# Depthwise convolution of a decoder trunk on TensorE: two tiles as diagonal products, or four tiles as packs of 32 channels by 4 shifts between the projection's chunks

## The chip, the cores and the metric

The kernel runs on one core of a Trainium2 chip. The metric is the device time of one execution in microseconds (us). The profile is one execution recorded by the hardware profiler; its rows name the engines PE (TensorE), PEld (TensorE's weight loads), DVE (VectorE), ACT (ScalarE), POOL (GpSimd) and SP (the queue that issues most transfers).

## The reference

There are two layers over 512 tokens of width 1024; only the first layer's branch matters here.

```python
def conformer_conv_branch(h, w_in, b_in, conv_w, conv_b, norm_g, norm_b, w_out, b_out):
    proj = h @ w_in + b_in                       # 1024 -> 3 x 2048
    val, glu_gate, z = jnp.split(proj, 3, axis=-1)
    u = val * jax.nn.sigmoid(glu_gate)
    u = lax.conv_general_dilated(u, conv_w[:, None, :], window_strides=(1,),
        padding=[(CONV_KERNEL - 1, 0)], dimension_numbers=('NWC', 'WIO', 'NWC'),
        feature_group_count=CONV_WIDTH) + conv_b # 31 taps, each channel by itself
    u = jax.nn.silu(layer_norm(u, norm_g, norm_b))
    u = u * jax.nn.silu(z)
    return u @ w_out + b_out
```

The rest (the residual's LayerNorm, then a latent attention layer with its projections) is the same in both kernels.

## The kernel before, in words

Data lie with channels on the 128 partitions and the 512 tokens along the row. The 2048 channels of the branch are 16 tiles `t` of 128 x 512; `u` holds them with 30 zero columns ahead (`PAD`).

**Chunks on PE.** One chunk `c` is 128 output columns of `w_in`: 24 matmuls of 128x512, since each float32 product is made of three (weights low part by data high, high by low, high by high). Chunks 0 to 31 alternate value (even) and gate (odd) of tiles 0 to 15, so tile `t` is complete after chunk 2t+1. Chunks 32 to 47 are z, called z0 to z15 below. A chunk's weights come by a transfer of SP into one of two `w_raw` slots, ACT rounds them to `w_hi`, POOL subtracts to get `w_lo` (`split_lo`), and PE waits for both. A `w_raw` slot is free when its `w_hi` and `w_lo` are made. After a gate chunk ACT makes `val` and `sig` and POOL multiplies them into `u` (`glu`).

**The convolution** of 31 taps per tile is dealt out to three places:

- DVE does the tiles in `VECTOR_TILES` (0, 1, 2, 4, 5, 6, 7, 8, 10, 11, 14, 15), one instruction a tap, two tiles in turn, with the partial sum in a PSUM bank; and the last 10 taps of tile 12.
- PE does 21 taps of tile 12 and all 31 of tile 13 (`convolve(m)`), each tap as a product with a diagonal matrix: 52 taps of 3 matmuls, all of them between chunk 31 and z0. POOL makes the high diagonals (`diag_hi`), ACT the low ones.
- Tiles 3 and 9 (`SHARED_TILES`) are multiplied tap by tap on ACT (`tap_product`) and added on POOL (`add_product`): 62 taps, dealt out over the steps of both engines.

**The mean.** The LayerNorm over channels needs the sum of all tiles. POOL sums 11 tiles (`pool_csum`), DVE the others, and when `csum` is ready PE multiplies it by ones after the sixth of the eight parts of z11 (`MEAN_AT = (11, 5)`, `sum_over_channels`). The rest of PE's queue stands behind that matmul. The sum of squares follows inside z14.

Every engine runs its own instructions in the order written and waits on semaphores; there is no scheduler. `tap_done` counts DVE's taps, and `whole_at()` says at which count a tile is whole.

Of the kernel before, what the change touches and what calls it, by code (L numbers as in the profile page):

```python
# [26 lines left out]
F32 = mybir.dt.float32  # L27
F32R = mybir.dt.float32r
# [12 lines left out]
PAD = TAPS - 1  # L41
N_HEADS = 16
# [71 lines left out]
def trunk_kernel(nc, x, positions, ln_g, ln_b, a_w_in, a_b_in, a_conv_w, a_conv_b, a_norm_g,  # L114
# [14 lines left out]
    with ExitStack() as ctx:  # L129
# [67 lines left out]
        cu_hi = [at(f"cu_hi{i}", reg_x, 4 * TILE + 544 * i, [P, SEQ + PAD], F32R) for i in range(2)]  # L197
        cu_lo0 = at("cu_lo0", reg_x, 4 * TILE + 1088, [P, SEQ + PAD], F32R)
# [7 lines left out]
        vec_raw = at("vec_raw", reg_acc, 4 * TILE, [V_ALL, P])  # L206
        pos_int = at("pos_int", reg_x, 8 * TILE - 512, [P, SEQ], I32)
# [5 lines left out]
        diag_hi = at("diag_hi", reg_z, 0, [P, TAPS, P], F32R)  # L213
        diag_lo = at("diag_lo", reg_z, TAPS * P, [P, TAPS, P], F32R)
# [95 lines left out]
        taps_hi_ready, taps_lo_ready, taps_ready = sem("taps_hi_ready"), sem("taps_lo_ready"), sem("taps_ready")  # L310
# [76 lines left out]
        SHARES_BEGIN = SHARED_TILES[0] + 2  # L387
# [61 lines left out]
        SECOND_BEGINS = 14  # L449
        POOL_SUM_BEGINS = 8  # L450
        POOL_SUM = MATRIX_TILES[1:] + SHARED_TILES + VECTOR_TILES[:8]

        def whole_at():

            first_tap = {t: 0 for t in VECTOR_TILES}
            first_tap[MATRIX_TILES[0]] = MATRIX_TAPS[0]
            coming, running, taken, done, slot, ends = list(first_tap), [None, None], [0, 0], 0, 0, {}
            while coming or running != [None, None]:
                if running[slot] is None and coming and (slot == 0 or done >= SECOND_BEGINS):
                    running[slot] = coming.pop(0)  # L460
                    taken[slot] = first_tap[running[slot]]
                if running[slot] is not None:
                    taken[slot] += 1
                    done += 1
                    if taken[slot] == TAPS:
                        ends[running[slot]] = done
                        running[slot] = None
                slot = 1 - slot
            return ends

        def pair_taps(t):

            n = max(0, t - SHARES_BEGIN)
# [1612 lines left out]
```

## Time and profile before

| | |
|---|---|
| median of 3 runs | 820.56 us (820.43 to 822.16) |
| span of the profiled execution, first to last instruction | 818.7 us |
| time of the profiled execution beside its span | the profile states none; the median lies 1.86 us above the span |
| PE / DVE / ACT / POOL busy, of the span | 99% / 74% / 48% / 66% |
| granted TensorE clock, mean | 0.999 of full |

The span is counted from the first instruction, and all times below are from there. The busy time of a PE matmul includes its drain, which overlaps the next one: the distance between the starts of two matmuls is shorter than the mean duration in a row.

### The profile page before, as it was taken

To read this page: it belongs to the slowest core of one execution; us is meant where nothing else is said; L and a number is where in the kernel's file an instruction comes from. 1 tells how busy PE (TensorE), PEld (TensorE's weight loads), DVE (VectorE), ACT (ScalarE), POOL (GpSimd) and SP (SyncE) were. 2 spreads that over 40 slices of the span, in tenths; PEclk is the share of its full clock that TensorE was granted. 3 is DMA by queue.
4 is the path that set the end of the run, shared out by engine and by line. 5 is a ranking of instruction groups with operands and counts; after the bars stand their busy time and mean duration, and the time that the engine had idled before them with its cause. 6 is when DMAs were issued, how large, how long until landed. Compare 5 with 4: busy or idle time off the path is not lost.

```text
span 818.7 us, 11442 instructions
## 1 busy us (share of the span) xinstructions
PE 807.0 (99%) x3891; PEld 681.3 (83%) x3891; DVE 602.9 (74%) x1026; ACT 395.5 (48%) x711; POOL 542.3 (66%) x335
## 2 busy tenths in 40 slices
PE   8999999999999999999999999999999999999996
PEld 8888888888888887888898788888888888888885
DVE  2699999999999978994833192037788888876217
ACT  4654444455564368622342444256666766664210
POOL 4677999995999954594355438426877776387430
PEclk9999999999999999999999999999999999999999
DMA  6333333330032324444233335115766664663412
GB/s 221 103 103 103 92 88 87 93 104 26 25 105 84 109 79 146 157 160 129 52 107 114 101 102 167 54 41 176 206 200 191 201 199 130 186 205 129 155 52 102
DMA packets 123019, 100.01 MB, mean 122 GB/s; under 512 B 15354, under 2 KB 107616, under 8 KB 122972
## 3 DMA queue, kind: packets, MB, share of 16 engines
q1 hardware_dynamic: 122972, 99.42, 40.4%
q8 instruction: 25, 0.41, 0.2%
q14 instruction: 22, 0.18, 0.1%
HBM read 82.36 MB, written 12.58 MB: 116 GB/s over the span
## 4 chain that ended last, share of the span: by engine, by line
PE 95%; DMA 2%; DVE 1%; ACT 0%; issue 0%; SPq 0%; DVEq 0%
PE bank L1694 91%; DMA x_in<-in_x_dram 1%; PE bank L1999 1%; PE bank L2000 1%; DMA prob_kept<-prob 1%; DMA prob_moved<-prob_kept 0%; PE bank L1873 0%; PE bank L1992 0%; DVE prob L1591 0%; PE bank L1926 0%; PE bank L1990 0%; PE bank L1808 0%; DVE prob L1596 0%; SPq L524 0%; ACT bank L1201 0%
## 5 line engine op out<-in xcount | busy, mean ns | idle before, releaser
L730 POOL TENSOR_TENSOR w_lo<-w_raw,w_hi 128x1024 fp32r<-128x1024 f32 x102 | 252.6, 2485 | 114.1 <-ACT w_hi L927 106.8
L1330 DVE SCALAR_TENSOR_TENSOR bank<-u,conv_w,bank 128x512 f32<-128x512 f32 x357 | 238.6, 747 | 0.5
L1694 PE MATMUL bank<-xt_hi,w_lo 128*128 128x512 f32 (+1 forms) x392 | 151.9, 388 | 0.0
L1694 PE MATMUL bank<-xt_hi,w_hi 128*128 128x512 f32 (+1 forms) x392 | 150.9, 385 | 0.0
L927 ACT ACTIVATE w_hi<-w_raw 128x1024 fp32r<-128x1024 f32 x102 | 106.3, 1054 | 92.2 <-PE bank L1694 29.8
L1694 PE MATMUL bank<-xt_lo,w_hi 128*128 128x512 f32 (+1 forms) x392 | 150.8, 385 | 0.0
L1694 PEld LDWEIGHTS bank<-xt_lo,w_hi 128*128 128x128 f32 x392 | 73.7, 188 | 15.0 <-issue 0.5
L1694 PEld LDWEIGHTS bank<-xt_hi,w_lo 128*128 128x128 f32 x392 | 73.7, 188 | 15.0 <-issue 0.5
L1694 PEld LDWEIGHTS bank<-xt_hi,w_hi 128*128 128x128 f32 x392 | 73.6, 188 | 14.7
L767 POOL TENSOR_TENSOR acc<-acc,tap_product 128x512 f32<-128x512 f32 x60 | 77.8, 1297 | 9.7 <-ACT tap_product L960 4.5
L1694 PE MATMUL bank<-ht_hi,w_lo 128*128 128x512 f32 (+1 forms) x208 | 76.4, 367 | 0.0
L1694 PE MATMUL bank<-ht_lo,w_hi 128*128 128x512 f32 (+1 forms) x208 | 75.8, 365 | 0.0
L1694 PE MATMUL bank<-ht_hi,w_hi 128*128 128x512 f32 (+1 forms) x208 | 75.8, 365 | 0.0
L886 POOL TENSOR_TENSOR pt_lo<-prob_moved,pt_hi 128x512 fp32r<-128x512 f32 (+1 forms) x64 | 57.7, 935 | 15.4 <-ACT pt_hi L1208 15.1
L855 POOL TENSOR_TENSOR bundle_lo<-bundle_raw,bundle_hi 128x1024 fp32r<-128x1024 f32 (+1 forms) x16 | 49.2, 3073 | 26.4 <-ACT bundle_hi L1135 26.4
L960 ACT ACTIVATE tap_product<-u,conv_w 128x512 f32<-128x512 f32 x60 | 42.0, 719 | 30.8 <-POOL acc L767 30.8
L1694 PE MATMUL bank<-w_hi,fg_lo 128*128 128x512 f32 x128 | 50.1, 391 | 0.7 <-issue 0.7
L1694 PE MATMUL bank<-w_hi,g_lo 128*128 128x512 f32 x128 | 50.1, 392 | 0.3 <-DVE g_lo L1422 0.3
L1694 PE MATMUL bank<-w_lo,g_hi 128*128 128x512 f32 x128 | 49.8, 389 | 0.0
L1694 PE MATMUL bank<-w_hi,g_hi 128*128 128x512 f32 x128 | 49.8, 389 | 0.0
L1694 PE MATMUL bank<-w_lo,fg_hi 128*128 128x512 f32 x128 | 49.8, 389 | 0.0
L1694 PE MATMUL bank<-w_hi,fg_hi 128*128 128x512 f32 x128 | 49.8, 389 | 0.0
(213 smaller groups left out, 1722.0 us busy)
## 6 DMA issues: line engine op xcount, KB each, us to landing
w_raw<-in_a_w_in_dram SPq DMA_DIRECT2D x48, 512.0 KB, 3.7
w_raw<-in_b_w_in_dram SPq DMA_DIRECT2D x20, 512.0 KB, 3.6
prob_kept<-prob SPq DMA_DIRECT2D x16, 640.0 KB, 3.1
prob_moved<-prob_kept SPq DMA_DIRECT2D x64, 160.0 KB, 3.2
w_raw<-in_a_w_out_dram SPq DMA_DIRECT2D x16, 512.0 KB, 4.0
w_raw<-in_b_w_out_dram SPq DMA_DIRECT2D x16, 512.0 KB, 3.5
bundle_raw<-in_b_w_uq_dram SPq DMA_DIRECT2D x16, 256.0 KB, 4.4
x_in<-in_x_dram SPq DMA_DIRECT2D x4, 512.0 KB, 5.8
```

The lines of the kernel that those rows point to most:

```text
L730: nc.gpsimd.tensor_tensor(w_lo[slot][:], w_raw[raw][:], w_hi[slot][:].bitcast(F32), ALU.subtract).then_inc(w_lo_ready, 1)
L767: nc.gpsimd.tensor_tensor(acc[:, t, :], acc[:, t, :], tap_product[n % 2][:], ALU.add).then_inc(product_added, 1)
L855: nc.gpsimd.tensor_tensor(bundle_lo[slot][part][:], bundle_raw[:, lo:hi], bundle_hi[slot][part][:].bitcast(F32), ALU.subtract).then_inc(bu ...
L886: nc.gpsimd.tensor_tensor(turned_block(pt_lo, b), moved_block(b), turned_block(pt_hi, b).bitcast(F32), ALU.subtract).then_inc(pt_lo_ready, 1)
L927: nc.scalar.activation(w_hi[slot][:], w_raw[raw][:], ACT.Copy).then_inc(w_hi_ready, 1)
L960: nc.scalar.activation(tap_product[n % 2][:], u[:, t, k:k + SEQ], ACT.Copy, scale=tap).then_inc(product_ready, 1)
L1330: nc.vector.scalar_tensor_tensor(out=inner[:] if k < TAPS - 1 else acc[:, t, :], in0=u[:, t, k:k + SEQ], scalar=conv_w[:, column:column + ...
L1694: last = nc.tensor.matmul(out_ap, a, b, start=(start and n == 0 and m == 0), stop=(stop and n == len(parts) - 1 and m == 2))
L1999: nc.tensor.matmul(total, stack[:, cut], keys(kr_lo[:]), start=False, stop=False)
L2000: nc.tensor.matmul(total, stack[:, cut], keys(kr_hi[:]), start=False, stop=True).then_inc(scores_done, 1)
```

## The change: four tiles on PE in packs, eleven on DVE, one shared

`MATRIX_TILES` becomes 1, 5, 9, 13, `SHARED_TILES` becomes 3 alone, and DVE has the other eleven tiles whole.

A tile on PE is cut into four packs of 32 channels. The 128 rows of the moving operand are those 32 channels at 4 successive shifts, so one matmul holds 4 taps of 32 channels for each of 4 column groups, which are 4 parts of the 31 taps. A pack takes two windows (`STEPS`), each with three matmuls; four packs make 24 matmuls a tile, 96 in all. They run in two halves of 12 after chunks 13 and 14, 21 and 22, 29 and 30, and z5 and z6.

To get the stacked rows, ACT rounds the tile to `cu_hi`, POOL makes `u_lo`, SP writes both to DRAM (`keep_u`) and reads them back in 8 transfers onto 32 partitions each (`stack_u`). POOL makes two matrices a tile (`pack_matrices`, 128x1024 each). ACT copies the packs out of PSUM and, from its own queue, writes them to DRAM (`keep_packs`), then brings three parts into the rows of `u` tiles 0, 2 and 4, whose taps are done, and the fourth into `acc` (`bring_parts`). DVE adds the three parts at their shifts onto `acc` (`add_part`, 3 instructions a tile): for the first three tiles after its taps 150, 222 and 294, for the last after all taps.

DVE splits tiles 0, 2, 4, 6 and 15 (`ALONE`) into taps 0 to 15 and 16 to 30, run in turn, and one addition joins them (`join_halves`). The chunk loops of PE and SP are written out. The two rounded tables of taps (`conv_w_hi`, `conv_w_lo`) are gone; four more transposes on PE after chunk 2 give the taps of the packs.

```diff
-        MATRIX_TILES = (12, 13)
-        MATRIX_TAPS = (21, TAPS)
+        MATRIX_TILES = tuple(range(MATRIX_COLUMN, CT, CT // TAP_ROWS))
+        BEGINS = (3, 7, 11, 15)
+        PACK_BANK = (6, 7)
-        SHARED_TILES = (3, 9)
+        SHARED_TILES = (3,)
-        PAIR_SHARE, MATRIX_SHARE, Z_SHARE = 3, (1, 1, 1, 9), 2
+        PAIR_SHARE = {6: 3, 7: 2, 8: 3, 10: 3, 11: 2, 12: 3, 14: 3, 15: 2}
+        Z_SHARE = {0: 2, 1: 2, 4: 2, 5: 2, 6: 2}
+        ALONE = (0, 2, 4, 6, 15)
+        ADD_PARTS_AT = (150, 222, 294)
...
+            def stack_after(c):
+                for m, begin in enumerate(BEGINS):
+                    n = c - 2 * begin
+                    if n == 3:
+                        keep_u(m)
+                    elif n in (5, 6):
+                        stack_u(m, 0, (0, 1) if n == 5 else (2, 3))
+                    elif n in (7, 8):
+                        stack_u(m, 1, (0, 1) if n == 7 else (2, 3))
...
@@ POOL, the z chunks @@
                 split_lo(Z0 + i, i % 2, i % SLOTS)
                 if i == 0:
                     glu(CT - 1, (CT - 1) % 2)
-                    for g in range(SHARED_SLOTS):
-                        conv_matrices(1, g)
-                        for n in matrix_taps(g):
-                            add_product(n)
+                if i in (2, 3):
+                    pack_matrices(len(MATRIX_TILES) - 1, i - 2)
                 for n in z_taps(i):
                     add_product(n)
...
@@ ACT @@
+            def bring_parts(m):
+                for i in range(2):
+                    act.wait_ge(part_written[i], 16 * (PACKS // 2) * (m + 1))
+                act.wait_ge(tap_done, whole_at()[PART_TILES[-1]])
+                wait(act, parts_added, (PARTS - 1) * m)
+                nc.scalar.dma_start(u[:, PART_TILES[0]:PART_TILES[-1] + 1:2, PAD:], parts_kept[m][0:PARTS - 1].rearrange("q p i -> p q i")
+                                    ).then_inc(parts_landed, 16)
+                nc.scalar.dma_start(acc[:, MATRIX_TILES[m], :], parts_kept[m][PARTS - 1]).then_inc(parts_landed, 16)
...
@@ DVE @@
+            def add_part(m, n):
+                t = MATRIX_TILES[m]
+                part = PARTS - 2 - n
+                shift = PART_SHIFT * (n + 1)
+                moved = u[:, PART_TILES[part], PAD - shift:PAD - shift + SEQ]
+                if n == 0:
+                    dve.wait_ge(parts_landed, 32 * (m + 1))
+                    nc.vector.scalar_tensor_tensor(out=acc[:, t, :], in0=acc[:, t, :], scalar=vec[:, V_CONVB + t:V_CONVB + t + 1],
+                                                   in1=moved, op0=ALU.add, op1=ALU.add).then_inc(parts_added, 1)
+                else:
+                    dve.wait_ge(parts_added, (PARTS - 1) * m + n)
+                    nc.vector.tensor_tensor(acc[:, t, :], acc[:, t, :], moved, ALU.add).then_inc(parts_added, 1)
...
@@ PE @@
-            for m in range(len(MATRIX_TILES)):
-                convolve(m)
+            def packs_after(c):
+                for m, begin in enumerate(BEGINS):
+                    if c - 2 * begin in (7, 8):
+                        half = c - 2 * begin - 7
+                        pack(m, 2 * half)
+                        pack(m, 2 * half + 1)
...
             for i in range(CT):
-                if i == 3:
-                    pe.wait_ge(pe_conv_kept, len(MATRIX_TILES))
                 columns(Z0 + i, i % SLOTS, i % 4, Z0 + i - 3, xt_hi, xt_lo, between.get(i))
+                packs_after(Z0 + i)
```

On DVE, in the middle of the taps, the kernel before alternates two tiles (`bank<-u,conv_w,bank` is a tap, `acc<-u,conv_w,bank` a tile's last, `TENSOR_SCALAR` its first) and adds whole tiles to the channel sum as they end (`bank<-acc`, `bank<-bank,acc`):

```order
L1322 TENSOR_SCALAR bank<-u,conv_w,vec 128x512
L1312 COPY bank<-acc 128x512
L1330 SCALAR_TENSOR_TENSOR bank<-u,conv_w,bank 128x512 x24
L1330 SCALAR_TENSOR_TENSOR acc<-u,conv_w,bank 128x512
L1330 SCALAR_TENSOR_TENSOR bank<-u,conv_w,bank 128x512
L1322 TENSOR_SCALAR bank<-u,conv_w,vec 128x512
L1314 TENSOR_TENSOR bank<-bank,acc 128x512
```

In the changed kernel, from the start of tiles 7 and 8 on:

```order
L1412 TENSOR_SCALAR bank<-u,conv_w,vec 128x512 x2
L1420 SCALAR_TENSOR_TENSOR bank<-u,conv_w,bank 128x512 x20
L1439 SCALAR_TENSOR_TENSOR acc<-acc,vec,u 128x512
L1420 SCALAR_TENSOR_TENSOR bank<-u,conv_w,bank 128x512 x2
L1443 TENSOR_TENSOR acc<-acc,u 128x512
L1420 SCALAR_TENSOR_TENSOR bank<-u,conv_w,bank 128x512 x2
L1443 TENSOR_TENSOR acc<-acc,u 128x512
L1420 SCALAR_TENSOR_TENSOR bank<-u,conv_w,bank 128x512 x34
L1420 SCALAR_TENSOR_TENSOR acc<-u,conv_w,bank 128x512 x2
```

Tiles 7 and 8 now begin at the same instruction, and three additions with both inputs in SBUF stand among the taps. At the end of the taps (tile 15 by halves) the changed kernel has this, where the one before had three channel sums among its taps and two behind the last:

```order
L1412 TENSOR_SCALAR bank<-u,conv_w,vec 128x512
L1416 TENSOR_SCALAR bank<-u,conv_w 128x512
L1420 SCALAR_TENSOR_TENSOR bank<-u,conv_w,bank 128x512 x27
L1420 SCALAR_TENSOR_TENSOR acc<-u,conv_w,bank 128x512
L1420 SCALAR_TENSOR_TENSOR bank<-u,conv_w,bank 128x512
L1428 TENSOR_TENSOR acc<-bank,acc 128x512
L1439 SCALAR_TENSOR_TENSOR acc<-acc,vec,u 128x512
L1443 TENSOR_TENSOR acc<-acc,u 128x512 x2
L1402 COPY bank<-acc 128x512
L1404 TENSOR_TENSOR bank<-bank,acc 128x512 x3
L1404 TENSOR_TENSOR csum<-bank,pool_csum 128x512
```

The last tile's three parts and all five channel sums stand in one chain behind tile 15.

On POOL, around the last product of `val` and `sig` (tile 15), the kernel before has the split of chunk z0, that product, four diagonals and 12 products, and only then the split of z1:

```order
L730 TENSOR_TENSOR w_lo_76<-w_raw_70,w_hi_72 128x1024
L742 TENSOR_TENSOR u<-val_82,sig_84 128x512
L779 TENSOR_TENSOR diag_hi<-ident,conv_w_hi 128x640
L767 TENSOR_TENSOR acc<-acc,tap_product_115 128x512
L779 TENSOR_TENSOR diag_hi<-ident,conv_w_hi 128x640
```

The changed kernel has there:

```order
L790 TENSOR_TENSOR w_lo_77<-w_raw_71,w_hi_73 128x1024
L802 TENSOR_TENSOR u<-val_83,sig_85 128x512
L828 TENSOR_TENSOR acc<-acc,tap_product_119 128x512
L828 TENSOR_TENSOR acc<-acc,tap_product_118 128x512
L790 TENSOR_TENSOR w_lo_78<-w_raw_72,w_hi_74 128x1024
L828 TENSOR_TENSOR acc<-acc,tap_product_119 128x512
```

The split of z1 now stands two products behind tile 15's `u`, and on PE chunk z0 follows chunk 31 directly.

## Rows read from the trace of the kernel before

**Rows 1.** Chain that ended last, in order of time: start, length, what.

```profile
23.43 263.56 PE bank L1694 x1158
286.99 1.09 PE bank L1801 x2
...
303.73 1.68 PE bank L1808 x16
```

**Rows 2.** Timeline of PE: start, us, instruction, and idle before.

```profile
22.76 0.59 PE L1720 MATMUL bank<-ident,taps_raw 124*128 124x124 f32 x4
23.18 0.25 PE L1723 MATMUL bank<-ident,vec_raw 102*128 102x102 f32 x1
...
186.54 0.39 PE L1694 MATMUL bank<-cu_hi,diag_lo 128*128 128x512 f32 x1
...
222.86 0.39 PE L1694 MATMUL bank<-xt_hi,w_lo 128*128 128x512 f32 x1
...
286.98 1.10 PE L1801 MATMUL bank<-csum,ones 128*128 128x512 f32 x2
```

**Rows 3.** Timeline of DVE, the taps and what follows them.

```profile
28.78 0.81 DVE L1322 TENSOR_SCALAR bank<-u,conv_w,vec 128x512 f32<-128x512 f32 x1 [2.36 <-POOL u L742]
...
61.57 0.74 DVE L1330 SCALAR_TENSOR_TENSOR acc<-u,conv_w,bank 128x512 f32<-128x512 f32 x1
...
102.51 0.74 DVE L1330 SCALAR_TENSOR_TENSOR acc<-u,conv_w,bank 128x512 f32<-128x512 f32 x1
...
285.35 0.69 DVE L1314 TENSOR_TENSOR bank<-bank,pool_csum 128x512 f32<-128x512 f32 x1
286.14 0.69 DVE L1314 TENSOR_TENSOR csum<-bank,acc 128x512 f32<-128x512 f32 x1
...
302.51 0.69 DVE L1387 TENSOR_TENSOR vsum<-bank,sq 128x512 f32<-128x512 f32 x1
```

**Rows 4.** Timeline of POOL.

```profile
111.35 1.29 POOL L742 TENSOR_TENSOR u<-val,sig 128x512 f32<-128x512 f32 x1 [0.71 <-ACT sig L936]
112.60 4.19 POOL L767 TENSOR_TENSOR acc<-acc,tap_product 128x512 f32<-128x512 f32 x3
116.75 4.75 POOL L730 TENSOR_TENSOR w_lo<-w_raw,w_hi 128x1024 fp32r<-128x1024 f32 x2
...
187.51 1.29 POOL L742 TENSOR_TENSOR u<-val,sig 128x512 f32<-128x512 f32 x1 [2.17 <-ACT sig L936]
...
219.62 2.40 POOL L730 TENSOR_TENSOR w_lo<-w_raw,w_hi 128x1024 fp32r<-128x1024 f32 x1
221.98 2.73 POOL L767 TENSOR_TENSOR acc<-acc,tap_product 128x512 f32<-128x512 f32 x2
```

**Rows 5.** Timeline of ACT.

```profile
23.38 1.07 ACT L1002 ACTIVATE conv_w_hi<-bank 128x496 fp32r<-128x496 f32 x1 [2.87 <-PE bank L1720]
24.24 0.30 ACT L1004 ACTIVATE vec<-bank 128x102 f32<-128x102 f32 x1
```

**Rows 6.** Groups of DVE and PE by form: count, busy us and mean ns.

```profile
L1330 DVE SCALAR_TENSOR_TENSOR bank<-u,conv_w,bank 128x512 f32<-128x512 f32 x357 | 238.6, 747 | 0.5
...
L1633 DVE TENSOR_TENSOR fg_lo<-gate,fg_hi 128x512 fp32r<-128x512 f32 x16 | 22.6, 1454 | 6.3 <-ACT fg_hi L1226 6.3
L1551 DVE TENSOR_TENSOR lat<-lat,k_swap 128x512 f32<-128x512 f32 x1 | 0.7, 677 | 0.0
L1694 PE MATMUL bank<-cu_hi,diag_hi 128*128 128x512 f32 x52 | 20.5, 394 | 0.0
```

**Rows 7.** Timeline of DVE and POOL where both read SBUF back to back.

```profile
362.62 2.76 DVE L1455 TENSOR_TENSOR angle_c<-angle_c,turns 128x512 f32<-128x512 f32 x1
...
362.25 2.58 POOL L850 TENSOR_TENSOR res<-res,ln_rows 128x1024 f32<-128x1024 f32 x1
364.80 2.84 POOL L730 TENSOR_TENSOR w_lo<-w_raw,w_hi 128x1024 fp32r<-128x1024 f32 x1
```

**Rows 8.** DMA issues of the first projection's weights: count, KB, us to landing.

```profile
w_raw<-in_a_w_in_dram SPq DMA_DIRECT2D x48, 512.0 KB, 3.7
```

More of the change, by code:

```diff
@@ L515, in load_columns, with keep_u, stack_u @@
                              source[:, :, bass.ds(column, P)]).then_inc(w_landed[slot], 16)
-            def load_value_gate(j, first=0):
-                for s in range(first, ROUND):
-                    for w in range(2):
-                        raw_free(2 * ROUND * j + 2 * s + w)
-                        load_columns(w, w_in_a, w * CONV_WIDTH + (ROUND * j + s) * P)
+            def keep_u(m):
+                sp.wait_ge(cu_hi_ready, m + 1)
+                sp.dma_start(u_kept[m][0], cu_hi[:].bitcast(F32)).then_inc(u_written, 16)
+                sp.wait_ge(cu_lo_ready, m + 1)
+                sp.dma_start(u_kept[m][1], u_lo[:, MATRIX_TILES[m], :].bitcast(F32)).then_inc(u_written, 16)
+            def stack_u(m, low, shifts):
+                if shifts[0] == 0 and not low:
+                    sp.wait_ge(u_written, 32 * (m + 1))
+                    wait(sp, pack_done, PACKS * m)
+                stack, landed = ((stacked_hi, stacked_hi_landed), (stacked_lo, stacked_lo_landed))[low]
+                for j in shifts:
+                    columns = slice(FIRST_COLUMN + j, FIRST_COLUMN + j + STACK)
+                    sp.dma_start(stack[PACK * j:PACK * (j + 1), :, :].bitcast(F32),
+                                 u_kept[m][low][:, columns].rearrange("(g c) x -> c g x", c=PACK)).then_inc(landed, 16)
+            def stack_after(c):
[7 more added lines that the diff above has]
+                        stack_u(m, 1, (0, 1) if n == 7 else (2, 3))
             for r in range(RT):
@@ L1013, in _ @@
                 value_gate(t)
+                if t == 2:
+                    act.wait_ge(stack_turned, 1)
+                    act.wait_ge(consts_ready, 6)
+                    for j in range(SHIFTS):
+                        nc.scalar.activation(stack_rows(stack_hi, j), turned_stack(j), ACT.Copy).then_inc(stack_hi_ready, 1)
             def keep_z(i):
@@ L1788, in _, with pack @@
-            value_gate(0)
-            with pe.Fori(1, ROUNDS) as j:
-                value_gate(j)
-            for m in range(len(MATRIX_TILES)):
-                convolve(m)
+            def pack(m, g):
+                n = PACKS * m + g
+                if g == 0:
+                    pe.wait_ge(matrix_hi_ready, m + 1)
+                    pe.wait_ge(matrix_lo_ready, m + 1)
+                    pe.wait_ge(stacked_hi_landed, 16 * SHIFTS * (m + 1))
+                wait(pe, pack_kept, n - 1)
+                out = bank[PACK_BANK[n % 2]]
+                windows = [slice(REACH * s, REACH * s + SEQ) for s in range(STEPS)]
+                for s, window in enumerate(windows):
+                    nc.tensor.matmul(out[:], matrix_lo[:, g, s, :], stacked_hi[:, g, window], start=s == 0, stop=False)
+                    nc.tensor.matmul(out[:], matrix_hi[:, g, s, :], stacked_hi[:, g, window], start=False, stop=False)
+                if g == 0:
+                    pe.wait_ge(stacked_lo_landed, 16 * SHIFTS * (m + 1))
+                for s, window in enumerate(windows):
+                    last = nc.tensor.matmul(out[:], matrix_hi[:, g, s, :], stacked_lo[:, g, window], start=False,
+                                            stop=s == STEPS - 1)
+                last.then_inc(pack_done, 1)
```

359 lines of the change are left out of this document (204 added, 155 removed).

## Prediction

> **What bounds the kernel now.** I read the busy shares first: PE 99%, so a matmul saved should be time saved. The chain that ended last says the same: up to 286.99 us it is one run of matmuls [rows 1]. The price of one must come from the distance of starts, not from the mean duration: the 156 convolution matmuls run from 186.54 to 222.86 [rows 2], 36.32 us or 0.233 each, where the row of busy time says 394 ns [rows 6]. In the projections it is 263.56 / 1158 = 0.228 each, so a chunk of 24 takes 5.46 us [rows 1].
>
> Then I looked at who else arrives at 286.98, where PE multiplies `csum` for the mean. DVE's last channel sum starts at 286.14 and takes 0.69, so `csum` is whole at 286.83, 0.15 us before PE uses it [rows 2, 3]. From its first tap at 28.78 DVE has next to no idle time. Two engines therefore end at the same place, and a shorter PE alone buys nothing: whichever comes last at the mean sets it. Everything behind the mean is the same work in both kernels. It follows the mean on both engines: the sum of squares needs `vsum` at 303.20 and PE asks for it about 303.6 [rows 1, 3]. So I forecast the new instant of the mean and shift the rest.
>
> **PE's arrival at the mean.** 156 matmuls go, 96 come: 36.32 - 96 x 0.233 = 36.32 - 22.35 = 13.97 us less. Four transposes like those at 22.76 add the 0.42 from there to the next instruction [rows 2]. That gives 286.98 - 13.97 + 0.42 = 273.4.
>
> The diagonals' 36 us also covered something. Chunk 31 will end at 186.54 + 0.42 + 72 x 0.233 = 203.7, and z0 follows at once and ends 5.46 later, at 209.2. POOL made tile 15's `u` by 188.80, 2.26 us after chunk 31's end [rows 4]; that is 206.0 in the changed kernel. Behind it stand two products and then the split of z1: 2.7 and 2.4 us [rows 4], so z1's `w_lo` is ready at 211.1. PE waits 1.9 us there; before, this split was made at 219.62 in the shade of the diagonals. PE's arrival: 275.3.
>
> Elsewhere I find no PE wait. A pair of chunks costs POOL 4.75 (two splits), 1.29 and at most 4.19 us of a 10.9 us pair [rows 4]. The two matrices replace the products in their pair; I put them at 2.4 each like any 128x1024 operation, or 4.8 against 4.2. The transfers of a tile are issued over several chunks, and a load of 512 KB takes 3.7 us to land [rows 8]; the last stack of a tile is issued when POOL has split the weights of two chunks before, about two chunks (11 us) before its pack. Two or three such transfers fit, so I price them at nothing. If that cover is gone each late tile costs PE directly. ACT's new waits (for packs, for written parts) hold back `w_hi` of a chunk that PE needs about three chunks later; the longest, at z9 for the packs after z6, leaves over 10 us.
>
> **DVE's arrival.** Two tiles in turn take 102.51 - 61.57 = 40.94 us for 62 taps, 20.5 a tile [rows 3]. A dependent operation starts 0.79 after the one before (285.35 to 286.14 [rows 3]), so a joined pair of halves costs 20.5 + 0.9 = 21.4.
>
> - ACT no longer makes `conv_w_hi`, so its next row can start about 0.7 earlier (23.5 for 24.24 [rows 5]), and DVE's first tap at 28.0 for 28.78.
> - Tiles 0, 2, 4 and 6 at 21.4, with 0.8 for four short splits of the pack taps: 28.0 + 85.6 + 0.8 = 114.4. Each tile's `u` arrives just before its turn.
> - Tiles 7 and 8 begin together, and tile 8 isn't there. Its `u` was written at 112.64 [rows 4]; with the transposes and one tile's packs (24 x 0.233 = 5.6) it is at 118.7. DVE waits 4 us until 118.8 with one tap done.
> - Then 40.94 - 0.7 = 40.2 for the remaining 61 taps, and three additions at 0.65: 161.0. Two more such blocks at 42.9 give 246.8, tile 15 by halves 268.2.
> - Behind it a chain of eight operations, three parts and five sums: 7 x 0.79 + 0.69 = 6.2, so `csum` at 274.4, and PE 0.15 later: 274.6.
>
> So far the two engines meet at 275, a gain of nearly 12 us. But the twelve additions of parts are of a kind that no tap is: both inputs lie in SBUF. Such an addition takes 677 ns with POOL idle and 2,762 in a stretch where POOL subtracts and adds without pause, POOL's own operation growing from 2.4 to 2.6 and 2.8 [rows 6, 7]. The 16 of `fg_lo`, with POOL busy part of the time, take 1,454 in the mean [rows 6]. The bounds for one wait are therefore 0 and 2,762 - 677 = 2.1 us. I take what a chance arrival finds: POOL's pair of chunks has two operations of 2.4 and four of 1.3 in 10.9 us, so the mean remainder is (2 x 2.4² + 4 x 1.3²) / (2 x 10.9) = 0.84 us. Nine additions stand there: 7.6. The last three meet a POOL with one split a chunk: 2.4² / (2 x 5.46) = 0.53 each, 1.6. Together 9.2 us, near the 0.77 each of `fg_lo`. The twelve can't recover it elsewhere, since from 118.8 on DVE is never ahead of its tiles. DVE's arrival: 274.6 + 9.2 = 283.8.
>
> The Trainium skill ("SBUF — State Buffer", Who interferes with whom) says that a VectorE instruction with two SBUF inputs and a GpSimd instruction that reads SBUF exclude each other, the later one waiting for the whole of the other. By that rule the taps (one input in PSUM) are free and only these additions pay, up to one full POOL operation of 2.4 each. The trace agrees: 747 ns for the taps throughout, 2,762 for the addition above [rows 6, 7].
>
> **Sum.** The mean moves from 286.98 to 283.8, 3.2 us earlier; PE waits there some 8 us. The span becomes 815.5, and with the 1.9 us between span and median the time is 820.56 - 3.2 = **817.3 us**.
>
> **Rivals.**
>
> - *The additions don't wait* (they happen to fall into POOL's gaps, or only the first of each group waits). Then both engines arrive at 275.3, PE last because of z1: 820.56 - 11.7 = 808.9. For it: POOL idles 0.7 us before each `glu`, and the two engines fall into a rhythm rather than meeting by chance. Against: nine of twelve stand where POOL is about 93% busy. Chance 0.15.
> - *The time doesn't move.* The waits total 10.7 to 14 us, 0.9 to 1.15 an addition, for instance because each one held back starts POOL's next operation together with DVE's next taps, and the next addition then meets its remainder. Time 819 to 822. Chance 0.2.
> - *Slower: every addition pays for nearly a whole POOL operation.* It decides from 14 us in all, 1.17 each. At the upper bound, 12 x 2.1 = 25 us, the mean comes at 299.8 and the time is 833.4. For it: the last three are a dependent chain, and POOL slips in between them; the row of 2,762 is of that kind. Against: in the first nine there are two taps (1.3 us) between additions, so a split of 2.4 has half run out. Chance 0.1.
> - *Slower or level: transfers.* A tile adds 0.56 MB written (`u` high and low), 2.2 MB stacked and twice 1.05 MB of parts, so four add 19 MB in some 220 us, partly in the queue of the weights. The loads are 3.7 us to landing [rows 8]. A delay before chunk 17 shifts `u` of tile 8 and so DVE one for one; a later one only uses PE's 8 us. To undo the gain it takes 3 us before chunk 17. Chance 0.05.
>
> **How the numbers follow.** The forecast's own case (waits of 5 to 10.7 us in all) has 0.5 and gives 813 to 819. With the first rival that makes faster 0.65; within 0.2% (1.6 us, about what a measurement of this kernel can tell) 0.2; slower 0.15. The range leaves out the far upper bound and reaches down to the case without waits: 809 to 822.5. Below it the one way is that z1 doesn't stall either, 13.5 us at most (807.0).
>
> **What the changed profile would show.** PE: a wait of about 8 us before the mean's matmul, released by DVE's `csum`, and one of about 1.9 us at z1 on `w_lo`; pack matmuls 0.23 apart. DVE: 4 us idle on `u` before tile 8; the twelve additions at 1.2 to 1.9 us in the mean against 0.69 without POOL; the last tap near 276. POOL: splits that begin late by one DVE addition. If the additions show 0.7 us and PE's only wait is at z1, the second step of DVE's sum was wrong. The forecast is also wrong if the tap itself gets slower than 0.66, since 341 of them stand in the chain: 0.01 us more is 3.4 us.

## The result: slower by 0.6%, and the profile after

The changed kernel takes 826.49 us in the median of 9 runs (823.07 to 829.26), the kernel before 821.76 (818.75 to 823.04); the ratio is 1.0061, 95% interval 1.0042 to 1.0081. I had forecast 817.3 and a range up to 822.5.

What PE and DVE waited for between 28 and 300 us, in the profile of the changed kernel (us in total, times, longest):

```profile
PE bank L1896 <- ACT part_out L1004: 5.1, 1, 5.1
PE bank L1811 <- ACT w_hi L983: 4.8, 1, 4.8
PE bank L1929 <- DVE csum L1404: 1.3, 1, 1.3
...
DVE bank L1412 <- POOL u L802: 7.3, 2, 3.7
DVE acc L1439 <- DMA acc<-parts_kept: 6.3, 1, 6.3
```

L1896 is a pack, L1811 a chunk, L1929 the mean. The end of the stretch on DVE, the successor of [rows 3]:

```profile
278.84 0.69 DVE L1428 TENSOR_TENSOR acc<-bank,acc 128x512 f32<-128x512 f32 x1
285.79 2.78 DVE L1439 SCALAR_TENSOR_TENSOR acc<-acc,vec,u 128x512 f32<-128x512 f32 x1 [6.25 <-DMA acc<-parts_kept]
288.60 1.42 DVE L1443 TENSOR_TENSOR acc<-acc,u 128x512 f32<-128x512 f32 x2
...
293.14 0.69 DVE L1404 TENSOR_TENSOR csum<-bank,pool_csum 128x512 f32<-128x512 f32 x1
```

DVE has ended tile 15 and stands 6.25 us: the last tile's parts have not come back from DRAM. The chain that ended last says why (start, length, what):

```profile
255.65 3.64 DMA w_raw<-in_a_w_in_dram
...
260.28 1.07 ACT part_out L1004 x2
...
261.45 10.22 DMA parts_kept<-part_out
...
271.75 0.61 ACT part_out L1004
...
281.00 4.76 DMA acc<-parts_kept
285.79 2.79 DVE acc L1439
```

Read it upwards. The parts land 4.8 us after they are fetched. They are fetched at 281.00, when the four packs have been written. ACT can copy out the last two packs only when the first two have left the two `part_out` buffers; their write counts 10.22 us in the chain. And the first two came late because ACT stood before the weights of z9.

The same wait stands inside the first projection. ACT at tile 5's packs, behind chunks 21 and 22 (in brackets, idle time before):

```profile
148.70 1.09 ACTq L1008 DMA_DIRECT2D parts_kept<-part_out  x2
149.89 0.69 ACT L989 ACTIVATE val<-bank,vec 128x512 f32<-128x512 f32 x1 [0.73 <-PE bank L1811]
155.15 0.60 ACT L1004 ACTIVATE part_out<-bank 128x512 f32<-128x512 f32 x1 [4.57 <-DMA parts_kept<-part_out]
159.16 0.60 ACT L1004 ACTIVATE part_out<-bank 128x512 f32<-128x512 f32 x1 [3.42 <-DMA parts_kept<-part_out]
...
160.35 0.69 ACT L995 ACTIVATE sig<-bank,vec 128x512 f32<-128x512 f32 x1 [0.59 <-ACT part_out L1004]
```

Behind the copies stands `sig`, and POOL's gate product waits for it. At tile 9's packs, the next ones, it is `sig` of tile 15 that comes late (first three rows). POOL then idles 8.6 us ahead of tile 15's `u`, which starts at 211.40; the split of z1 is behind that, and PE behind the split:

```profile
206.30 0.60 ACT L1004 ACTIVATE part_out<-bank 128x512 f32<-128x512 f32 x1 [6.27 <-DMA parts_kept<-part_out]
209.44 0.60 ACT L1004 ACTIVATE part_out<-bank 128x512 f32<-128x512 f32 x1 [2.54 <-DMA parts_kept<-part_out]
210.64 0.69 ACT L995 ACTIVATE sig<-bank,vec 128x512 f32<-128x512 f32 x1 [0.60 <-ACT part_out L1004]
...
211.40 1.30 POOL L802 TENSOR_TENSOR u<-val,sig 128x512 f32<-128x512 f32 x1 [8.60 <-ACT sig L995]
212.67 2.68 POOL L828 TENSOR_TENSOR acc<-acc,tap_product 128x512 f32<-128x512 f32 x2
215.30 2.36 POOL L790 TENSOR_TENSOR w_lo<-w_raw,w_hi 128x1024 fp32r<-128x1024 f32 x1
...
217.76 0.77 PE L1811 MATMUL bank<-xt_hi,w_lo 128*128 128x512 f32 x1 [4.83 <-ACT w_hi L983]
218.33 0.63 PE L1811 MATMUL bank<-xt_lo,w_hi 128*128 128x512 f32 x1
218.75 0.63 PE L1811 MATMUL bank<-xt_hi,w_hi 128*128 128x512 f32 x1
```

The wait row names `w_hi`, but the instruction that ended last before 217.76 is POOL's split (215.30 + 2.36 = 217.66). Behind the wait the matmuls are 0.42 apart, not 0.23, for 5 us, and behind the wait in the packs for 6 us. Windows on PE (width, PE busy, granted clock as a share of full speed, DMA share, GB/s) show it at both long waits:

```profile
210.00:215.00 5.00, 2.94 (x13) 1.00 0.22 54
215.00:220.00 5.00, 2.24 (x5) 0.59 0.31 102
220.00:225.00 5.00, 5.00 (x18) 0.73 1.05 301
225.00:230.00 5.00, 5.00 (x24) 1.00 1.11 271
255.00:260.00 5.00, 0.80 (x4) 1.00 0.36 105
260.00:265.00 5.00, 4.09 (x10) 0.53 0.43 121
```

A stretch of the lower level (1.2 GHz) followed each of these two idle times. It cost some 2.3 us more after the first (11 matmuls, 217.76 to 222.59) and 2.9 after the second (14 matmuls, 260.91 to 267.05), against 0.23 each.

The last rows are the groups of DVE's additions (count, busy us, mean ns, idle before) and the transfers:

```profile
L1443 DVE TENSOR_TENSOR acc<-acc,u 128x512 f32<-128x512 f32 x8 | 12.5, 1556 | 0.1
L1439 DVE SCALAR_TENSOR_TENSOR acc<-acc,vec,u 128x512 f32<-128x512 f32 x4 | 6.6, 1647 | 6.3 <-DMA acc<-parts_kept 6.3
...
w_raw<-in_a_w_in_dram SPq DMA_DIRECT2D x48, 512.0 KB, 4.3
...
stacked_lo<-u_kept SPq DMA_DIRECT2D x16, 264.0 KB, 7.6
```

The twelve additions take 19.0 us; at 0.73 and 0.68 they would take 8.4. The excess is 10.7 us.

**One number for the comparisons.** The first product matmul starts at a different time in each profile, since the input lands when it lands (11.44 before, 14.02 after). So I take the start of the mean's matmul less that: 286.98 - 11.44 = 275.5 before, 293.97 - 14.02 = 280.0 after, 4.4 us later, close to the difference of the medians (4.7). From the mean's matmul to the end both take the same, 531.7 and 531.6.

### The profile page after: what moved, and what is told of

Read it like the earlier page. It is cut to its first block, busy times and chain, and to the rows that moved or that the text cites. A ratio compares the mean times of both kernels' runs of the same rounds, so it can differ in the third digit from the quotient of the medians.

```text
span 825.6 us, 11113 instructions
## 1 busy us (share of the span) xinstructions
PE 801.6 (97%) x3835; PEld 675.8 (82%) x3835; DVE 597.4 (72%) x1005; ACT 369.5 (45%) x651; POOL 514.2 (62%) x309
## 4 chain that ended last, share of the span: by engine, by line
PE 69%; POOL 11%; issue 8%; DMA 8%; DVE 2%; ACT 2%; SPq 1%; DVEq 0%; POOLq 0%; ACTq 0%
PE bank L1811 65%; POOL w_lo L790 4%; DMA w_raw<-in_a_w_in_dram 4%; POOL acc L828 4%; DMA parts_kept<-part_out 2%; POOL u L802 1%; DMA x_in<-in_x_dram 1%; DMA prob_kept<-prob 1%; PE bank L2126 1%; PE bank L2127 1%; DMA acc<-parts_kept 1%; PE bank L1829 0%; POOL bundle_lo L911 0%; PE bank L2000 0%; POOL u_lo L845 0%
## 5 line engine op out<-in xcount | busy, mean ns | idle before, releaser
L1420 DVE SCALAR_TENSOR_TENSOR bank<-u,conv_w,bank 128x512 f32<-128x512 f32 x314 | 208.7, 744 | 0.0
L1811 PE MATMUL bank<-xt_hi,w_lo 128*128 128x512 f32 (+1 forms) x392 | 153.8, 392 | 5.3 <-ACT w_hi L983 4.8
L1811 PE MATMUL bank<-xt_lo,w_hi 128*128 128x512 f32 (+1 forms) x392 | 152.2, 388 | 0.0
L1811 PE MATMUL bank<-xt_hi,w_hi 128*128 128x512 f32 (+1 forms) x392 | 151.7, 387 | 0.0
L1811 PEld LDWEIGHTS bank<-xt_hi,w_lo 128*128 128x128 f32 x392 | 74.6, 190 | 21.5 <-ACT w_hi L983 5.2
L1811 PEld LDWEIGHTS bank<-xt_lo,w_hi 128*128 128x128 f32 x392 | 74.5, 190 | 15.2 <-issue 0.5
L1811 PEld LDWEIGHTS bank<-xt_hi,w_hi 128*128 128x128 f32 x392 | 74.4, 190 | 15.1
L1811 PE MATMUL bank<-ht_hi,w_lo 128*128 128x512 f32 (+1 forms) x208 | 76.4, 367 | 0.0
L1811 PE MATMUL bank<-ht_lo,w_hi 128*128 128x512 f32 (+1 forms) x208 | 75.8, 365 | 0.0
L1811 PE MATMUL bank<-ht_hi,w_hi 128*128 128x512 f32 (+1 forms) x208 | 75.8, 365 | 0.0
L802 POOL TENSOR_TENSOR u<-val,sig 128x512 f32<-128x512 f32 x16 | 21.6, 1353 | 47.4 <-ACT sig L995 47.4
L1811 PE MATMUL bank<-w_hi,fg_lo 128*128 128x512 f32 x128 | 50.1, 391 | 0.7 <-issue 0.7
L1811 PE MATMUL bank<-w_hi,g_lo 128*128 128x512 f32 x128 | 50.1, 392 | 0.4 <-DVE g_lo L1539 0.2
L1811 PE MATMUL bank<-w_lo,fg_hi 128*128 128x512 f32 x128 | 49.8, 389 | 0.0
L1811 PE MATMUL bank<-w_hi,g_hi 128*128 128x512 f32 x128 | 49.8, 389 | 0.0
L1811 PE MATMUL bank<-w_hi,fg_hi 128*128 128x512 f32 x128 | 49.8, 389 | 0.0
L1811 PE MATMUL bank<-w_lo,g_hi 128*128 128x512 f32 x128 | 49.8, 389 | 0.0
L1587 DVE SCALAR_TENSOR_TENSOR bank<-res,bank 128x512 f32<-128x512 f32 x16 | 11.0, 689 | 51.5 <-PE bank L1811 51.5
```

Of the source, the lines that this page charges most:

```text
L802: nc.gpsimd.tensor_tensor(u[:, bass.ds(t, 1), PAD:].rearrange("p o n -> p (o n)"), val[slot][:], sig[slot][:], ALU.mult).then_inc(u_ready, 1)
L1420: nc.vector.scalar_tensor_tensor(out=inner[:] if k < TAPS - 1 else acc[:, t, :], in0=u[:, t, k:k + SEQ], scalar=conv_w[:, column:column + ...
L1587: nc.vector.scalar_tensor_tensor(out=total[:], in0=rows_half, scalar=scale, in1=total[:], op0=ALU.mult, op1=ALU.add).then_inc(y_step, 1)
L1811: last = nc.tensor.matmul(out_ap, a, b, start=(start and n == 0 and m == 0), stop=(stop and n == len(parts) - 1 and m == 2))
```

## The experiments

Each was measured with runs of the kernel before beside it; the ratio is to those. Their medians lay between 820.93 and 822.09, so medians of two rows that differ by 1 us say little: by the ratios e1 gains 6.6 us on the changed kernel, by the medians 7.3. The last column comes from one profile each. e3, e6 and e11 leave out part of the computation (see e3).

| kernel | median us | ratio (95%) | first product to mean |
|---|---|---|---|
| changed kernel | 826.49 | 1.0061 (1.0042 to 1.0081) | 280.0 |
| e1 four buffers | 819.24 | 0.9981 (0.9964 to 0.9998) | 272.5 |
| e2 stacks moved | 826.86 | 1.0070 (1.0057 to 1.0083) | 281.2 |
| e3 one SBUF input | 820.30 | 1.0001 (0.9986 to 1.0016) | 275.1 |
| e4 = e1 + e2 + packs first | 817.51 | 0.9962 (0.9950 to 0.9975) | 269.1 |
| e5 last tile earlier | 821.77 | 0.9998 (0.9982 to 1.0014) | 275.4 |
| e6 = e4 + one SBUF input | 814.06 | 0.9900 (0.9872 to 0.9928) | 266.8 |
| e7 = e4 + halves | 819.58 | 0.9977 (0.9961 to 0.9993) | 274.3 |
| e8 packs first | 825.92 | 1.0047 (1.0025 to 1.0069) | 279.9 |
| e9 = e4 + e5 | 817.55 | 0.9941 (0.9920 to 0.9962) | 269.1 |
| e10 = e9 + halves | 815.90 | 0.9930 (0.9909 to 0.9951) | 270.7 |
| e11 = e10 + one SBUF input | 810.88 | 0.9871 (0.9849 to 0.9894) | 266.0 |
| e12 = e10, parts summed in PSUM | 809.94 | 0.9862 (0.9838 to 0.9886) | 265.5 |
| e13 = e1 + e5 + halves | 815.98 | 0.9925 (0.9902 to 0.9949) | 271.7 |

**e1, four output buffers.**

```diff
-        part_out = [at(f"part_out{i}", cos_at, i * TILE, [P, SEQ]) for i in range(2)]
+        part_out = [at(f"part_out{i}", base, offset, [P, SEQ]) for i, (base, offset) in enumerate(
+            ((cos_at, 0), (cos_at, TILE), (reg_e, 0), (conv_w_at, CT * TAPS + 2 * P + PACK)))]
...
-                    wait(act, part_written[i], 16 * (n // 2))
+                    wait(act, part_written[g], 16 * m)
```

> Four buffers for the packs' outputs instead of two, so that the second half of a tile's packs never waits for the first half to be written. Transfer theory (the 5 us come from waits that the transfers cause on ScalarE, PE and in front of VectorE's last sums): ScalarE's waits of 4.6, 6.3 and 3.0 us for those writes go, POOL's idle stretches of 7.9, 8.6 and 6.7 us before its gate products shrink to 2 or less, and the last parts land some 3 us earlier: 822 to 824 us instead of 826.5. Port theory (the 5 us are VectorE's additions that wait for POOL): nothing moves, 826 to 827. If only the end of the last tile matters: 823.5, the same 3 us, whatever POOL's stretches do.

It gained 7.3 us, more than I had expected of it. ACT's waits for the writes are gone:

```profile
148.03 1.08 ACTq L1010 DMA_DIRECT2D parts_kept<-part_out  x2
149.48 0.69 ACT L990 ACTIVATE val<-bank,vec 128x512 f32<-128x512 f32 x1 [0.99 <-PE bank L1813]
150.81 0.60 ACT L1006 ACTIVATE part_out<-bank 128x512 f32<-128x512 f32 x1 [0.65 <-PE bank L1903]
152.19 0.60 ACT L1006 ACTIVATE part_out<-bank 128x512 f32<-128x512 f32 x1 [0.78 <-PE bank L1903]
```

`sig` waits for PE now, as before the change. PE's wait at z1 fell from 4.8 to 1.8 us, DVE's for the last parts from 6.3 to 1.8. POOL still idles 31.9 us before its gate products after 60 us (36.6 in the changed kernel), but because PE isn't ready: my expectation took idle time for harm.

The rows divide the gain up. Counted from the first product, PE goes on with the last tile's packs 5.8 us earlier (254.39 - 13.32 against 260.91 - 14.02), most of it by the shorter wait at z1 (3.0 us) and the stretch of the lower clock that is gone with it (2.3). The last two packs are written 10.0 us earlier (261.69 against 272.38 in the two chains, less the same starts), so 4.2 more than that; the wait for a buffer is missing there. But these writes and the reading back then take 3.8 us longer, so the parts land 6.2 us earlier (265.6 for 271.8). The other 1.3 us of the 7.5 in the last column is the first of the last three additions, 1.47 us instead of 2.78.

**e2, stacks behind each pair of loads.**

```diff
-                    elif n in (5, 6):
-                        stack_u(m, 0, (0, 1) if n == 5 else (2, 3))
-                    elif n in (7, 8):
-                        stack_u(m, 1, (0, 1) if n == 7 else (2, 3))
+                    elif m == 3 and n in (5, 6, 7, 8):
+                        stack_u(m, n // 7, (0, 1) if n % 2 == 1 else (2, 3))
+                    elif m < 3 and n in (5, 7):
+                        stack_u(m, n // 7, (0, 1, 2, 3))
```

> For the first three tiles the eight stack transfers no longer stand between the two weight loads of a pair, four stand behind each pair. Transfer theory in its first form (weights stuck behind stacks): ScalarE's waits of 5.9 and 6.1 us for weights go, PE's wait of 4.8 us near the second chunk of the last projection shrinks, 824 to 826. If only the end of the last tile matters, or the port theory holds: 826 to 827, since the last tile keeps its order.

No change (826.86). ACT's waits for weights did shrink from 55.8 to 48.3 us and PE's near z1 from 4.8 to 3.6, but the last tile's parts landed no earlier (DVE waits 10.0 us for them), and they set the mean. Loads do get stuck behind stacks: in the changed kernel's trace one among the last tile's stacks, which e2 leaves in place, took 9.6 us. For the first three tiles they aren't what costs.

**e3, one SBUF input.**

```diff
-                                                   in1=moved, op0=ALU.add, op1=ALU.add)
+                                                   in1=other[:], op0=ALU.add, op1=ALU.add)
...
-                    nc.vector.tensor_tensor(acc[:, t, :], acc[:, t, :], moved, ALU.add)
+                    nc.vector.tensor_tensor(acc[:, t, :], acc[:, t, :], other[:], ALU.add)
```

`other` is the PSUM bank of the tap before, and DVE also waits for that tap. The kernel leaves out the adding of the parts; the number of operations and the waits for the parts stay.

> The twelve additions of parts read a PSUM bank in place of the moved parts, with the same waits: the parts are not added, the output differs, and each addition has one SBUF input. Port theory: each takes about 0.75 us instead of 1.6 in the mean, VectorE is 8 to 10 us earlier at its last sums, and the time falls to 817 to 819. Transfer theory: VectorE then waits the longer for the last parts, which land at the same instant; only the three additions behind them get shorter, by up to 2 us: 824 to 826.5.

Both theories missed: 820.3, 6.2 us under the changed kernel. The additions did shrink, and DVE did wait the longer for the parts:

```profile
L1444 DVE TENSOR_TENSOR acc<-acc,bank 128x512 f32<-128x512 f32 x8 | 5.5, 683 | 0.2
L1440 DVE SCALAR_TENSOR_TENSOR acc<-acc,vec,bank 128x512 f32<-128x512 f32 x4 | 3.0, 744 | 11.8 <-DMA acc<-parts_kept 11.8
```

But the parts landed earlier too: 279.93 - 11.16 = 268.8 us after the first product, against 285.79 - 14.02 = 271.8. My reading is that the exclusion has two sides, and that POOL's side, its splits and so ACT's copies, feeds the parts: PE's wait at z1 is 2.6 us here, not 4.8. No run separates that way from others.

**e4, all three orders.** e1 and e2, and for the last tile ACT keeps a pack before it waits for the next weights:

```diff
             for i in range(CT):
+                if i in (9, 10):
+                    keep_packs(3, i - 9)
                 z_split(i)
...
-                if i in (9, 10):
-                    keep_packs(3, i - 9)
```

> Four output buffers, stacks moved as in the run before last, and for the last tile ScalarE keeps the packs before it splits the next chunk's weights. Transfer theory: PE's wait of 5.1 us in the last tile's packs goes, the parts land before VectorE has finished tile 15 (279.5 in the profile of after), the channel sum follows 6 to 8 us later, the mean comes at 287 to 288 and the time is 819.5 to 821.5. Port theory alone: 826 to 827. If the stacks of the last tile still hold back the weights: 822 to 824.

DVE goes from tile 15 (ended 274.2) straight to the parts; PE's wait in the packs is gone and it stands 5.0 us before the mean. 817.51: 0.4% faster than the kernel before, and 2 us under what I expected. The twelve additions took 15.1 us here, not 19.0, which none of these edits aims at.

**e5, the last tile one pair of chunks earlier**, on the changed kernel:

```diff
-        BEGINS = (3, 7, 11, 15)
+        BEGINS = (3, 7, 11, 14)
...
-                if i in (2, 3):
-                    pack_matrices(len(MATRIX_TILES) - 1, i - 2)
+                if i in (1, 2):
+                    pack_matrices(len(MATRIX_TILES) - 1, i - 1)
...
-                if i in (2, 11):
+                if i in (2, 9):
                     bring_parts(2 if i == 2 else 3)
-                if i in (9, 10):
-                    keep_packs(3, i - 9)
+                if i in (7, 8):
+                    keep_packs(3, i - 7)
```

> The changed kernel with two output buffers as it is, and only the fourth tile's work (its split, its stacks, its packs, the return of its parts) one pair of chunks earlier, 10.9 us. If only the end of the last tile matters: its parts land some 10 us earlier, before VectorE has finished tile 15, VectorE's wait of 6.3 us goes, and the time falls by 7 to 8 us to 818 to 820. If the waits all along the way cost time (the late gate products, the weights behind the stacks): 821 to 824, since those stay. Port theory: 824 to 826.

It gained 4.7 us; 821.77 lies in the second range, that of the waits along the way. DVE's wait for the parts is gone, but PE's wait behind the late gate product is still there, 5.4 us. The twelve additions took 20.9 us here against 19.0, so some of what the edit freed went into the port.

**e6, e4 with e3's edit.**

> The run with all the edits on transfers, and the twelve additions reading a PSUM bank in place of the moved parts (the parts are not added, the output differs). In that run the additions took 4 x 1.48 and 8 x 1.13 us, 6.6 us more than at 0.73 and 0.68, and PE stood 5.0 us before the mean. If these 6.6 us are waits for POOL's port and VectorE now sets the mean: VectorE 6.6 us earlier, PE then sets it at about 276.5, 4.5 to 5 us earlier: 812 to 813.5. If something else holds the channel sum (the parts' landing, POOL's own sum): 816 to 818 as before.

814.06, between the two ranges and nearer to the first. DVE ended tile 15 at 268.07, but then waited for the parts:

```profile
272.27 0.75 DVE L1442 SCALAR_TENSOR_TENSOR acc<-acc,vec,bank 128x512 f32<-128x512 f32 x1 [4.20 <-DMA acc<-parts_kept]
```

So 4.2 of the 6.6 us by which the additions are shorter (15.1 to 8.5) went into the next wait, and DVE, not PE, still set the mean.

**e7, tiles 7 and 8 by halves**, on e4:

```diff
-        ALONE = (0, 2, 4, 6, 15)
+        ALONE = (0, 2, 4, 6, 7, 8, 15)
```

> The run with all the edits on transfers, and tiles 7 and 8 each by halves instead of in turn with each other, so that VectorE has a whole tile to do before tile 8 must be there. The wait of 3.4 us for tile 8 goes, two joins of 0.69 and 0.2 of start come, 1.8 us: if VectorE's chain sets the mean, 1.6 us earlier, 815.5 to 816.5. If the wait only moves to the next tile (10): 817.5 or more.

A miss of the first branch: 819.58, 2 us slower than e4 (5 by the last column). The wait for tile 8 went, but the parts landed at 275.14, 2.2 us later than DVE had taken them in e4 if both are counted from the first product. DVE waited 6.5 us for them, the last three additions took 5.7 us where they had taken 2.8, and PE waited 7.2:

```profile
284.85 2.05 PE L1931 MATMUL bank<-csum,ones 128*128 128x512 f32 x2 [7.22 <-DVE csum L1406]
285.91 1.42 PE L1813 MATMUL bank<-xt_hi,w_lo 128*128 128x512 f32 x1
287.13 0.63 PE L1813 MATMUL bank<-xt_lo,w_hi 128*128 128x512 f32 x1
```

**e8, only ACT's order for the last tile**, on the changed kernel:

> The changed kernel with one line moved: for the last tile ScalarE keeps a pack before it waits for the next chunk's weights, not behind. If the 5.1 us of PE in the last tile's packs come from that order: they go, the last parts are written and land 4 to 5 us earlier, and the time is 821 to 822.5. If ScalarE's wait for the written first half takes it over: 825 to 826.5.

Its second branch came: 825.92. PE's wait in the packs fell from 5.1 to 1.5, DVE's for the parts grew from 6.3 to 8.7. PE's 5.1 us at that place were not on the path that sets the mean.

**e9, e4 and e5 together.**

> All the edits on transfers, and the fourth tile's work 10.9 us earlier as well. In the run with the edits on transfers alone VectorE went from tile 15 to the last parts without a gap (274.2), so the parts were just in time: if VectorE's own work sets the mean there, nothing is left to gain, 817 to 818.5. If the last parts' landing sets it in most executions: 815 to 816.5.

817.55, level with e4: the parts are there early now, and DVE's own work sets the mean (PE waits 2.0 us for it).

**e10, e9 with tiles 7 and 8 by halves.**

> The run before this one, with tiles 7 and 8 by halves. With the last tile at its old place this edit brought VectorE to the end of tile 15 at 268.6 and then into a wait of 6.5 us for the last parts. If the parts' landing is what held it: they land near 263 now, the channel sum ends at 275 to 276, and PE, which reaches the mean at 275 to 277, sets it: 812 to 814. If the port or another engine takes the place of that wait: 816 to 819.

815.90, between the two ranges (814 ends the first, 816 begins the second). DVE has `csum` at 278.82 and PE asks for it at 281.67 only: PE is last, held by 3.1 us in the packs. ACT copied the packs behind its tap products, and these waited for POOL (1.8 us before one of them), in a place where DVE adds parts:

```profile
230.28 3.41 POOL L829 TENSOR_TENSOR acc<-acc,tap_product 128x512 f32<-128x512 f32 x2 [0.21 <-ACT tap_product L1048]
...
236.01 3.16 POOL L829 TENSOR_TENSOR acc<-acc,tap_product 128x512 f32<-128x512 f32 x2
...
233.78 2.82 DVE L1445 TENSOR_TENSOR acc<-acc,u 128x512 f32<-128x512 f32 x1
```

The same pairs of additions on POOL take 2.73 in e12, where DVE's leave the port alone.

**e11, e10 with e3's edit.**

> The run before this one, with the additions of parts reading a PSUM bank in place of the moved parts (the parts are not added, the output differs). VectorE is then some 6 us earlier than PE. If PE's work alone sets the mean by then: the time of the run before within 1.5 us, 811 to 813.5, and PE has no wait for the channel sum. If VectorE still set it there: 4 to 6 us less than the run before.

PE has no wait for the channel sum, as the first branch says; it came to 810.88, but 5 us under e10, the size the second branch gave. Both engines were freed: the pack wait fell from 3.1 to 0.2 us, and with it went the stretch of the lower clock behind it (240.46 to 244.87 in e10, 1.4 us more for 13 matmuls).

**e12, the parts really summed, in a PSUM bank.** Bias first, two additions in bank 7, the last one to SBUF; the second pack of the next tile waits until the bank is read. A tile's four operations follow four taps in a row, not every second one.

```diff
+                if n == 0:
+                    nc.vector.tensor_scalar(bank[SUM_BANK][:], acc[:, t, :], vec[:, V_CONVB + t:V_CONVB + t + 1], None,
+                                            ALU.add).then_inc(parts_added, 1)
+                else:
+                    nc.vector.tensor_tensor(acc[:, t, :] if n == PARTS - 1 else bank[SUM_BANK][:], bank[SUM_BANK][:], moved,
+                                            ALU.add).then_inc(parts_added, 1)
```

> The run with tiles 7 and 8 by halves and the fourth tile earlier, and the parts summed in a PSUM bank that the packs leave free: bias, then two additions there, the last one back to SBUF. Four operations a tile instead of three, each with one SBUF input. If the waits of the additions are for POOL's port: each takes 0.7 to 0.8 us, the 4.9 us above 0.73 and 0.68 go and 16 x 0.66 for 12, 2.7 us, come; PE, which reached the mean at 277.6 in the run without parts, sets it: 811 to 813. If one SBUF input meets POOL as well: 815 to 818.

809.94 us, 1 us under the range, 1.4% under the kernel before and 2% under the changed one, and the whole computation is in it. Its additions:

```profile
L1446 DVE TENSOR_TENSOR bank<-bank,u 128x512 f32<-128x512 f32 x8 | 5.5, 688 | 0.1
...
L1440 DVE TENSOR_SCALAR bank<-acc,vec 128x512 f32<-128x512 f32 x4 | 3.0, 742 | 0.0
```

and the one wait that PE has left between 60 and 300 us:

```profile
PE bank L1815 <- issue: 3.0, 2, 1.8
```

The profile names no releaser, but these two waits stand ahead of z1 and z2, and both times PE goes on 0.1 us after POOL's split of that chunk ends (at 210.28 and 217.23). For z1:

```profile
207.91 2.37 POOL L791 TENSOR_TENSOR w_lo<-w_raw,w_hi 128x1024 fp32r<-128x1024 f32 x1
210.38 0.47 PE L1815 MATMUL bank<-xt_hi,w_lo 128*128 128x512 f32 x1 [1.78 <-issue]
```

The first is the stall that the prediction had at z1. The second, 1.3 us, came with e5's edit, which puts one of the last tile's matrices between the two splits.

**e13, three edits only.** Four buffers, last tile earlier, halves; stacks and ACT's order as in the change.

> The changed kernel with three edits only: four output buffers, the fourth tile earlier, tiles 7 and 8 by halves. The stacks keep their place between the weight loads and ScalarE keeps the packs behind the next weights. If those two orders cost nothing once the buffers are there and the last tile is early: 815 to 817 like the run that has them changed as well. If they cost: 818 to 820, with waits of PE on ScalarE's weights or packs in the last projection.

815.98, level with e10. Once the buffers are there and the last tile is early, the two orders cost nothing that the medians show.

## Why the prediction was wrong, step by step

1. **PE's work** (156 to 96 matmuls, 0.233 each): right. In e12, where PE waits only for the splits of z1 and z2 (3.0 us), the mean comes at 265.5 after the first product. My arrival without the z1 stall was 273.4 - 11.44 = 262.0, and 262.0 + 3.0 = 265.0.
2. **The stall at z1, 1.9 us**: the right mechanism. It is 1.8 us in e1, e4, e6 and e7, and in e9 to e13 as well, where the profile calls it issue. In the changed kernel it is 4.8, because tile 15's `u` is made by 212.70 (211.40 + 1.30) where I had 206.0 + 2.6 (the later start) = 208.6, while PE itself was 1.1 us behind my working.
3. **"Elsewhere I find no PE wait"**: wrong. There are 5.1 us in the last tile's packs, and two stretches of the lower clock of 2.3 and 2.9 us. I also let PE wait 8 us at the mean and shifted the rest unchanged. In the changed kernel that wait is only 1.3 and the rest did stay the same, but where PE waited 2.7 to 7.2 us there (e2, e4, e6, e7, e8) the rest took 532.9 to 534.1 us instead of 531.6. So my own case would have cost some 2 us that I had left out.
4. **"ACT's new waits ... hold back `w_hi` of a chunk that PE needs about three chunks later"**: this is one of the two places where it failed. I looked at what ACT's weights copy can bear and not at what else stands behind: `sig`, and so `u` and POOL's splits. ACT waited 24.8 us in 7 times for writes to DRAM, which I hadn't priced. e1 takes just this wait away and gains 7.3 us; PE comes to the last tile's packs 5.8 us earlier by it.
5. **"so I price them at nothing"**: I counted transfers into the stacks, and these were harmless (e2, e13). The parts' way back, written, read, then needed by DVE, appears nowhere in my sum, and this is the step that the time hangs on: 13.4 us from the last write (272.38) to the addition (285.79), begun 7.1 us before DVE had ended tile 15. DVE stood 6.3 us for it; e5, which starts it earlier, gains 4.7. The edits overlap: e1 and e5 gain 7.3 and 4.7 alone, while e13, with both and the halves, gains 10.5.
6. **DVE without port waits**: right. Its first tap is at 30.78 (28.0 + 2.6 = 30.6), tile 7 begins at 117.44 (114.4 + 2.6 = 117.0), the wait for tile 8 is 3.7 (I had 4), a tap 744 ns. Tile 15 ends at 279.5; by my working 268.2 + 2.6 is 270.8, and the waits of the nine additions before it, 8.6 us by their rows, make 279.4 (I had 7.6 for them).
7. **Port waits, 9.2 us**: 10.7 in this profile. That they come from the second SBUF input is shown by e3 and e12 (0.68 to 0.75 us with one). The closeness is partly luck: the same twelve additions exceed 8.4 us by 6.5 in e13 and by 12.5 in e5, and where DVE meets POOL changes with every edit. The Trainium skill ("SBUF — State Buffer", Who interferes with whom) has each of the two engines wait for the other; I used half of it. The trace agrees: POOL's pair of additions takes 3.41 us beside DVE's in e10 and 2.73 in e12. POOL's loss, and through it ACT's and PE's, is in no term of my sum. e10 to e11 is 5.0 us, of which PE's pack wait is 2.9 and the lower clock behind it 1.4.

With 5 in the sum DVE's arrival becomes 283.8 + 2.6 (start) + 6.3 (parts) = 292.7, and `csum` was whole at 293.8. The rest is covered by the port, 10.7 for 9.2. The wait for a buffer (4) acts through it, by making the parts late. The rival "slower or level: transfers" had 0.05 and was what happened, but by another way than I gave it: not bytes before chunk 17, but a buffer that isn't free and a round trip that ends behind tile 15.

What stays open: why two writes take 10 us, by themselves or because of the transfers beside them; and whether the parts came 3 us earlier in e3 only by way of POOL. No run separates either.

## What to carry to other kernels

When a change sends results through DRAM and back, put the round trip (write, wait, read) into the sum as a term with a place where it ends, and ask of each buffer on the way what stands behind the instruction that waits for it. Where two engines exclude each other, price both sides, and look for the form of the operation that takes one operand from PSUM. And where several waits overlap, taking one away shows the next: e6 and e7 moved a wait, and the same edits paid once the last tile was early (e10 to e12).

## What the runs showed of the hardware

- Two writes of 256 KB to DRAM took long to be counted as done. In the changed kernel the pair in the chain at 261.45 took 10.2 us, and the pairs issued from 148.70 and 197.43 ended ACT's second wait at 159.16 and 209.44, 10.5 and 12.0 us later. A load of 512 KB took 4.3 us in the median of the same profile. The writes were not timed with the other queues quiet.
- In the 5 us windows with the ends of the waits of 4.8 and 5.1 us PE ran at a granted 0.59 and 0.53, and the matmuls were 0.42 apart for 4.8 and 6.1 us. After the waits of 1.3, 1.7 and 1.7 us at the mean (changed kernel, e3, e5) they are 0.23 apart again from the second one of the next chunk on. After 2.0 us in e9 and 2.7 us in e6 a stretch at 0.42 followed.
- DVE's addition with two SBUF inputs took 0.67 to 2.83 us, and POOL's pair of additions beside it 3.41 instead of 2.73; with one input from PSUM DVE's took 0.68 to 0.75 in all 12 or 16 cases.
